# States stored by SP, the sample tile's rows loaded by ScalarE, a product step and a set of masks moved, in a two-layer decoder step

## The reference

```python
for l in range(2):
    h = rmsnorm(x, norm_mix[l]); u, q, k, v, g = split(h @ w_in[l])         # w_in: 1024 x 2560
    pool_out = pool_mix(u, ...)
    s_new = s * gamma**8 + (k * k_decay).T @ v      # per head (4) and sample sequence (8): 128 x 128
    x = x + concat(pool_out, silu(g) * groupnorm(o)) @ w_out[l]
    hf = rmsnorm(x, norm_ffn[l])
    gates = top1_group_then_top2_experts(hf @ w_rg + b, hf @ w_re + b)      # 16 experts
    x = x + sum(gates[:, e] * (silu(hf @ w_gate[e]) * (hf @ w_up[e])) @ w_down[e] for e in range(16))
y = rmsnorm(x, norm_final)
# outputs: y_prompt, y_sample, the pooling buffers, and the retention states of prompt and sample
```

## Time and profile before

| | |
|---|---|
| time, median of 3 runs | 867.52 us (865.8 to 870.74) |
| the profiled execution's own time | 869.52 us |
| its span | 867.7 us |
| mean granted TensorE clock | 0.992 |
| TensorE busy | 843.0 us, 97% of the span |
| VectorE, ScalarE, GpSimd busy | 603.6, 479.4, 316.3 us |
| moved by DMA | 186.29 MB, mean 215 GB/s |

### The profile page before, as it was taken

How to read it: one execution, slowest core, us unless ns; L and a number is a source line. 1 busy time by engine, 2 the same in 40 slices (tenths; PEclk the granted TensorE clock), 3 DMA queues, 4 the chain that set the end, 5 groups by cost and what they waited for, 6 DMA issues and landing times.

```text
span 867.7 us, 12277 instructions
## 1 busy us (share of the span) xinstructions
PE 843.0 (97%) x4254; PEld 671.3 (77%) x4254; DVE 603.6 (70%) x953; ACT 479.4 (55%) x817; POOL 316.3 (36%) x203
## 2 busy tenths in 40 slices
PE   8999999999998999999899999999999999999994
PEld 5787888888866888888478888888877678888851
DVE  3435546555677999998664455655647799999956
ACT  3633442612456888887544333352335498888853
POOL 0014993301021477521100199702101237776110
PEclk9999999999989999999999999999999999999998
DMA  8622222324938999995764222321387698999838
GB/s 292 167 74 81 75 71 85 99 62 145 415 112 307 362 327 388 385 379 207 276 170 157 71 82 62 97 63 61 97 328 285 214 411 307 368 387 382 309 141 285
DMA packets 69439, 186.29 MB, mean 215 GB/s; under 512 B 15724, under 2 KB 26476, under 8 KB 61050
## 3 DMA queue, kind: packets, MB, share of 16 engines
q1 hardware_dynamic: 54714, 151.16, 49.7%
q0 software_dynamic: 10944, 25.19, 8.3%
q10 hardware_dynamic: 3728, 9.26, 2.8%
HBM read 170.56 MB, written 29.91 MB: 231 GB/s over the span
## 4 chain that ended last, share of the span: by engine, by line
PE 86%; DVE 6%; DMA 3%; ACT 2%; issue 1%; SPq 0%; ACTq 0%; POOLq 0%; DVEq 0%
PE ps L420 15%; PE ps L424 11%; PE ps L423 11%; PE ps L1254 9%; PE ps L1256 9%; PE ps L1255 9%; PE ps L422 3%; PE ps L1261 3%; PE ps L1232 2%; PE ps L1456 2%; DMA back<-y_d 1%; PE ps L1396 1%; DMA hg<-xn_d,rowidx 1%; PE ps L1421 1%; PE ps L1267 1%
## 5 line engine op out<-in xcount | busy, mean ns | idle before, releaser
L420 PE MATMUL ps<-wh,hT 128*128 128x512 f32 x480 | 194.0, 404 | 3.3 <-DVE lT L1784 2.6
L758 POOL DMA_INDIRECT y_d<-y,rowidx x32 | 118.5, 3702 | 118.1 <-DVE y L1870 118.1
L1850 DVE TENSOR_TENSOR gul<-wgu,eh 128x1024 fp32r<-128x1024 f32 x128 | 150.3, 1215 | 5.1 <-ACT eh L968 5.0
L424 PE MATMUL ps<-wh,lT 128*128 128x512 f32 x384 | 150.1, 391 | 0.0
L423 PE MATMUL ps<-wl,hT 128*128 128x512 f32 x384 | 150.0, 391 | 0.0
L1841 DVE SCALAR_TENSOR_TENSOR wl<-raw,gcol,wh 128x512 fp32r<-128x512 f32 x80 | 76.8, 964 | 81.4 <-ACT wh L941 81.2
L968 ACT ACTIVATE eh<-wgu 128x1024 fp32r<-128x1024 f32 x128 | 129.0, 1057 | 8.0 <-PE ps L1317 4.5
L420 PEld LDWEIGHTS ps<-wh,hT 128*128 128x128 f32 x480 | 90.3, 188 | 25.2 <-DVE lT L1784 5.2
L1254 PE MATMUL ps<-eh,hgTh 128*128 128x512 f32 x240 | 96.2, 401 | 0.4 <-issue 0.4
L941 ACT ACTIVATE wh<-raw,gcol 128x512 fp32r<-128x512 f32 x80 | 57.4, 721 | 67.9 <-PE ps L422 49.5
L1256 PE MATMUL ps<-eh,hgTl 128*128 128x512 f32 x240 | 93.7, 391 | 0.0
(11 more groups left out here) (231 smaller groups left out, 1577.2 us busy)
## 6 DMA issues: line engine op xcount, KB each, us to landing
wgu<-in_gate_up SPq DMA_DIRECT2D x64, 1024.0 KB, 8.5
wdn<-in_w_down SPq DMA_DIRECT2D x64, 512.0 KB, 12.1
raw<-in_w_in SPq DMA_DIRECT2D x80, 256.0 KB, 2.8
raw<-in_w_out SPq DMA_DIRECT2D x32, 256.0 KB, 3.0
back<-y_d SPq DMA_DIRECT2D x14, 512.0 KB, 7.5
xn_d<-xf ACTq DMA_DIRECT2D x10, 512.0 KB, 4.9
s<-in_state_ret POOLq DMA_DIRECT2D x8, 512.0 KB, 4.8
x<-in_x_prompt SPq DMA_DIRECT2D x4, 512.0 KB, 6.0
```

The costliest lines, as they stand in the source:

```text
L420: pe.matmul(out, both, w_h, start=first, stop=False)
L424: return pe.matmul(out, l[:, t * P:(t + 1) * P], w_h, start=False, stop=final)
L758: pool.indirect_dma_start(out=y_d, out_offset=bass.IndirectOffsetOnAxis(ap=rowidx[:, 1, e:e + 1], axis=0), in_=y[s][:, :], in_offset=None, ...
L1850: ve.tensor_tensor(gu_pair(gul, gul3, e, s, p), gu_pair(wgu, wgu3, e, s, p), eh[p][:, :].bitcast(F32), ALU.subtract).then_inc(glo, 1)
```

## The change

Four moves, no arithmetic added or removed.

- Late steps: their order becomes (2,0), (3,0), (3,1), (2,1). The step (2,1), which stood ahead of the wait for `taken`, comes behind the tables and behind (3,1), on TensorE and on ScalarE. The idle turns become 4 (from 5) ahead of `taken`, and 10 (from 18) behind the last step. SP stores head 3 first, then head 2.
- ScalarE: in the first layer `end_mask(L, 1)` comes behind the rounding of the next layer's blocks 0 to 2 (`w_hi`). VectorE makes the remainders of these blocks ahead of both `sample_state`, which stood around them.
- Last layer: the two row loads of tile 4 are issued by ScalarE behind `back[1]`, and no longer by SP ahead of those of tile 2.
- States of heads 0 and 1: stored by SP behind its row loads, in both layers (behind them in SP's program come, in the first layer, the next layer's blocks 4 and on). GpSimd no longer stores them and no longer waits for tile 2's rows.

```diff
--- before.py
+++ after.py
@@ -492,6 +492,7 @@
         B_Q, B_K, B_SC, B_O, B_KV = 6, 7, 6, 1, 7
         B_OT, B_ON = 0, (4, 5)
         B_END = ((3, 4), (1, 2))
+        LATE_STEPS = ((2, 0), (3, 0), (3, 1), (2, 1))
         B_LATE = ((4, 5), (6, 7))
         B_W = (2, 3, 2, 3, 2, 6, 7, 3, 2, 1, 0, 7, 3, 1, 2)
 
@@ -638,8 +639,8 @@
                     load_gain(NL)
                 sp.wait_ge(xn_st, 16 * NT * (L + 1))
                 sp.wait_ge(lg_mm, 2 * (L + 1))
-                for j in range(2):
-                    sp.wait_ge(s_late, 3 * L + (1, 3)[j])
+                for j in (1, 0):
+                    sp.wait_ge(s_late, 4 * L + (4, 3)[j])
                     sp.dma_start(o["new_ret_sample"][L, :, LATE + j].rearrange("b d e -> d b e"), s_out[j][:, :, :]).then_inc(late_st, 16)
                 for s in range(3):
                     sp.wait_ge(gat[s], 16 * used(L, s, 0))
@@ -681,8 +682,12 @@
                     if L + 1 == NL:
                         t = FINAL[t]
                     i = 2 * t + k
-                    n = tokens(t)
-                    sp.dma_start(back[i][0:n, :], y_d[k * TOK + t * P:k * TOK + t * P + n, :]).then_inc(third_ld if i == 2 else row_ld[t], 16)
+                    if t < LAST or L + 1 < NL:
+                        n = tokens(t)
+                        sp.dma_start(back[i][0:n, :], y_d[k * TOK + t * P:k * TOK + t * P + n, :]).then_inc(third_ld if i == 2 else row_ld[t], 16)
+                for h in range(LATE):
+                    sp.wait_ge(s_new, LATE * L + h + 1)
+                    sp.dma_start(o["new_ret_sample"][L, :, h].rearrange("b d e -> d b e"), s0_end[h][:, :, :]).then_inc(s0_st, 16)
             sp.wait_ge(out_st, 16 * NL)
             sp.wait_ge(upool_st, 32 * NL)
             sp.wait_ge(st_st, 16 * NL)
@@ -834,10 +839,6 @@
                 with pool.Else():
                     pool.wait_ge(t_mm, 2 * NE * (L + 1))
                 pool.wait_ge(t_mm, 2 * NE * (L + 1))
-                pool.wait_ge(row_ld[2], 16 + 32 * (L + 1))
-                for h in range(LATE):
-                    pool.wait_ge(s_new, LATE * L + h + 1)
-                    pool.dma_start(o["new_ret_sample"][L, :, h].rearrange("b d e -> d b e"), s0_end[h][:, :, :]).then_inc(s0_st, 16)
 
         def o_hi(eng, L, t):
 
@@ -901,11 +902,9 @@
 
             def late_state(L, h, n):
 
-                sc.wait_ge(skv_mm, 5 * L + (1 if h == 2 else 2 + n))
-                last = sc.activation(s_out[h - LATE][:, 4 * n:4 * n + 4, :], ps[B_LATE[h - LATE][n]][:, :].rearrange("p (b e) -> p b e", b=4),
-                                     ACT.Copy, scale=float(chunk_decay[1][h]))
-                if h == 3 or n:
-                    last.then_inc(s_late, 1)
+                sc.wait_ge(skv_mm, 6 * L + LATE_STEPS.index((h, n)) + 1)
+                sc.activation(s_out[h - LATE][:, 4 * n:4 * n + 4, :], ps[B_LATE[h - LATE][n]][:, :].rearrange("p (b e) -> p b e", b=4),
+                              ACT.Copy, scale=float(chunk_decay[1][h])).then_inc(s_late, 1)
 
             def gate_diagonals():
 
@@ -1146,7 +1145,6 @@
                 xn_out(L, LAST)
                 gu_hi(L, 0, 0, 0)
                 late_state(L, 2, 0)
-                late_state(L, 2, 1)
                 late_state(L, 3, 0)
                 sc.wait_ge(exp_in, L + 1)
                 sc.activation(gex[:, :, :], gds[:, :, :], ACT.Exp).then_inc(exp_out, 1)
@@ -1154,6 +1152,7 @@
 
                 table(ACT.Silu)
                 late_state(L, 3, 1)
+                late_state(L, 2, 1)
                 sc.wait_ge(xn_st, 16 * NT * (L + 1))
                 rows_hi(L, 0)
                 experts(sc, lambda e, s, n: expert(L, e, s, n))
@@ -1177,16 +1176,19 @@
                 with sc.Else():
                     sc.wait_ge(dpe, 2 * NE * (L + 1))
                 sc.wait_ge(dpe, 2 * NE * (L + 1))
-                end_mask(L, 1)
                 if L + 1 < NL:
                     for s in range(RAW):
                         w_hi(L + 1, s)
-                else:
+                end_mask(L, 1)
+                if L + 1 == NL:
                     table(ACT.Sqrt)
                     gate_diagonals()
                 for s in range(3):
                     sc.wait_ge(y_sc[s], 16 * EUSES[s] * (L + 1))
                 sc.dma_start(back[1][:, :], y_d[TOK:TOK + P, :]).then_inc(second_ld, 16)
+                if L + 1 == NL:
+                    for k in range(2):
+                        sc.dma_start(term(LAST, k)[0:NSAMP, :], y_d[k * TOK + LAST * P:k * TOK + LAST * P + NSAMP, :]).then_inc(row_ld[LAST], 16)
             last_root(0)
             for i, t in enumerate(FINAL):
                 if i + 1 < NT:
@@ -1463,9 +1465,7 @@
                 out, blocks = ps[B_LATE[h - LATE][n]][:, :], slice(4 * n, 4 * n + 4)
                 pe.matmul(out, ident, s0[h][:, blocks, :], start=True, stop=False)
                 pe.wait_ge(vb_done, NH * L + h - LATE + 1)
-                last = pe.matmul(out, kd_late[:, h - LATE, :], vb[h][:, blocks, :], start=False, stop=True)
-                if h == 3 or n:
-                    last.then_inc(skv_mm, 1)
+                pe.matmul(out, kd_late[:, h - LATE, :], vb[h][:, blocks, :], start=False, stop=True).then_inc(skv_mm, 1)
 
             def end_state(L, h):
 
@@ -1567,8 +1567,7 @@
                 logits(L, LAST)
 
                 late_state(L, 2, 0)
-                late_state(L, 2, 1)
-                idle_turns(3, 5)
+                idle_turns(3, 4)
                 pe.wait_ge(taken_done, L + 1)
                 for t in range(NT):
                     for u in range(t + 1):
@@ -1588,7 +1587,8 @@
                     last = pe.matmul(ps[2][:, 0:2 * NE], atslot[:, i, :], name_b[:, i, :, :], start=False, stop=(i == 2 * NT - 1))
                 last.then_inc(tab_mm, 1)
                 late_state(L, 3, 1)
-                idle_turns(3, 18)
+                late_state(L, 2, 1)
+                idle_turns(3, 10)
 
                 pe.wait_ge(gat[0], 16 * used(L, 0, 0))
                 rows_t(0, t_mm)
@@ -2019,7 +2019,7 @@
 
             def sample_state(L, h):
 
-                ve.wait_ge(skv_mm, 5 * L + 3 + h + 1)
+                ve.wait_ge(skv_mm, 6 * L + 4 + h + 1)
                 for n in range(2):
                     v = s0_end[h][:, 4 * n:4 * n + 4, :]
                     last = ve.scalar_tensor_tensor(out=v, in0=v, scalar=float(chunk_decay[1][h]),
@@ -2029,10 +2029,10 @@
             ve.wait_ge(ready0, 4)
             for L in range(NL):
                 if L:
-                    sample_state(L - 1, 0)
                     for s in range(RAW):
                         w_lo(L, s)
-                    sample_state(L - 1, 1)
+                    for h in range(LATE):
+                        sample_state(L - 1, h)
                     for s in range(RAW, EARLY[L]):
                         w_lo(L, s)
                     combine(L - 1, 0, 0)
```

## The result

The changed kernel takes 870.22 us (median of 17 runs, 868.04 to 873.18), the kernel before 867.52 (17 runs, 865.8 to 870.74): ratio 1.0034 [1.0023 to 1.0046], some 2.9 us slower. That is inside the 0.5% and inside the forecast's 863 to 871.5, but 3.1 us above its 867.1 and of the other sign: slower by 2.9, where the forecast had 0.4 faster. The profiled execution took 870.22 us with a span of 868.4; before, 869.52 and 867.7.

A forecast was written before the change was run, and what follows sets the result against it. TensorE was taken to bound the kernel, with 86% of the last-ending chain. End +0.6 (2.5 - 1.9), boundary 0, routing -2.0 or nothing gave 868.1 or 866.1 from the 867.52 median; the middle was 867.1 us, range 863 to 871.5.

The forecast's parts named there:

- Part 1, routing: Late step and turn leave the queue ahead of `taken`: 2.0 us gained in layer 0 at low clock, nothing in layer 1.
- The 1.0 that the number took from it: Routing's mean gain in us, between executions with the low-clock stretch (2.0 gained) and those without it (nothing).
- Part 2, boundary: Between layers, masks behind roundings: rows could come earlier, but idle turns hide the gain; 0, bounds -0.3 and +0.3 us.
- Part 3, the last store: At the end, states stored by SP let the last store land in 3.4 us, not 5.3: -1.9, bounds 0 and -2.6.
- The bounds of the sum for the end: Range given for the end's total, 2.5 - 1.9 = +0.6 us: from -1.3 to +2.5.
- Part 4, tile 4's rows: At the end, tile 4's rows on ScalarE's queue delay tile 3's products by 2.5 us; bounds 0 and 2.7.
- The rival of the low clock: Clock falls in new holes, costing 3.4 us at the end, 2.7 in layer 1's routing; 873.2 for both; chance 0.18.
- if the clock falls in a hole: Stated sign, without a size, that the forecast is wrong: TensorE's clock falling in one of its holes.
- It decides from about there: Low-clock rival's threshold: the clock was down after a 3.3 us hole at the end; the expected hole there was 3.2.
- The other two rivals: At the end: tile 3 not held up, 864.6 us, chance 0.17; last stores not relieved, 869.0 us, chance 0.15.

The follow-up runs named there:

- e2: Changed kernel with 30 idle turns instead of 16 ahead of tile 3's products; 869.26 us, ratio 1.0012 to the kernel before.
- e8: Kernel before with only the late-step reorder and the states stored by SP; 864.47 us, ratio 0.9957 to the kernel before.
- e1: Changed kernel with tile 4's row loads put back on SP's queue, ahead of tile 2's; 865.91 us, ratio 0.9979 to the kernel before.
- e15: Changed kernel itself, measured again in a later group of runs; 870.32 us, ratio 1.0034 to the kernel before.
- e12: Changed kernel with tile 4's rows back on SP and 9 of 25 boundary idle turns moved ahead of head 1's end products; 863.83 us, ratio 0.9956.
- e5: Kernel before with only the states of heads 0 and 1 stored by SP; 868.78 us, ratio 0.9988.
- e6: Kernel before with only tile 4's row loads moved to ScalarE's queue; 871.87 us, ratio 1.0026.
- e13: Kernel before with late-step reorder and SP-stored states, plus SP loading tile 4's rows ahead of tile 3's in the last layer; 868.88 us, ratio 1.0008.
- e3: Kernel before with only late step (2,1) moved behind the tables, with 4 and 10 idle turns; 868.29 us, ratio 0.999.
- e14: Kernel before with late-step reorder and SP-stored states, plus 13 idle turns instead of 4 ahead of positions; 866.42 us, ratio 0.9981.
- e9: Kernel before with only head 1's masks behind three roundings and remainders ahead of both sample states; 869.78 us, ratio 1.0012.

## Why the prediction was wrong in its sign

What failed is the pricing of TensorE's work behind two holes that the change opens. The sum took tile 3's products at the upper clock behind the rows' delay, and between the layers products and turns at 2.0 + 5.6, term 0. Measured, the fallen clock added 1.7 us at the end (`e2`) and some 1.4 at the boundary (`e8` against `e1`, `e15`). Together that is about the 3.1 us between forecast and result. The other differences are smaller and about cancel: the rows 0.8 later than taken, the last landing 0.6 earlier.

**Part 1, routing.** The step was right as drawn: positions came 0.05 behind `taken` (0.1 forecast), the gather 2.4 earlier (2.0), and where the clock was up TensorE had its hole (2.20 against 2.25 forecast). The 1.0 that the number took from it was not refuted: alone the part gave 0.1%, 0.9 us, with zero inside its interval. But it was right, if so, partly by luck. It was the middle between an execution that gains 2.0 and one that gains nothing. In the profiles a routing with the clock up mostly loses 0.8 to 1.5 behind the hole, which was left to a rival, and one with the clock low gains.

**Part 2, boundary.** This step failed. I wrote that masks end at 420.6 and that products and turns follow in 2.0 + 5.6, "Sum 0; bounds -0.3 and +0.3". The place and the order were right (the end products start 8.7 behind the last expert's last products, 8.8 forecast, and the turns took the chain from the rows), but the durations were those of the upper clock. I looked at two holes, and not at the one that this move opens between the 3 turns and the end products, 1.94. Behind it the pair took 9.1 instead of 7.5 in the changed kernel's profile and 10.8 in `e1`'s. `e8` against `e1` puts it at 1.4 us. `e12` shows that it goes when the hole is filled and turns are taken from behind; `e15`'s profile, where the clock stayed up after the same 1.94 and nothing was lost, shows that it is the clock. It fell in four of the five profiles that have this hole, and cost nothing in the fifth.

**Part 3, the last store.** Right in mechanism and nearly in size: 1.9 forecast, 2.3 alone, 2.5 in the changed kernel. Its landing was 2.8, under my 3.4. The medians of `e5` alone don't resolve it. Parts 1 and 3 together gave 0.43% where alone they gave 0.12% and 0.10%; the intervals allow both, so how the gain splits between them stays open. (The bounds of the sum for the end, -1.3 and +2.5, don't follow from those of its terms, which give -2.6 and +2.7; the measured +2.4 is inside both.)

**Part 4, tile 4's rows.** The mechanism was right, the size at the low end: tile 3's products came 3.3 later in the changed kernel's first profile, 2.6 in `e15`'s and 2.5 in `e6`, against the 2.5 taken (2.7 at most). `e13` confirms what the bound was built on, bytes at a low rate ahead of the tile that is wanted. The Trainium skill's rule ("DMA: Bandwidth & Descriptors", Rules for kernel authors) that more issuing engines bring no bandwidth agrees with the runs: 10.3 us with one queue (`e13`), 10.1 with two (`e6`). But the rows' lateness was not the whole price. The forecast moved tile 3's products later and left them at 3.67; they took 5.37, and the last store was issued 4.9 later, not 2.5.

**The rival of the low clock.** It had 0.18 and came true, in both places and in a third, and with it the sign "if the clock falls in a hole". "It decides from about there", 3.3 us, was wrong: holes of 1.9 and 2.2 preceded falls between the layers and in the routing. At the end the hole was 3.3 to 4.0, and the clock fell in each of the five profiles that have it. Its price was too high: 5.37 - 3.67 = 1.7 and not 3.4, because the clock was back after 3.4 us and not 6.7, and in the routing 0.8 to 1.5 and not 2.7. The other two rivals fell: tile 3 was held up, and the last store was relieved.

**The sum.** Forecast: 2.5 - 1.9 + 0 - 1.0 = -0.4. Measured in the places: the end +4.9 - 2.5, the boundary +1.4, the routing about -0.9 (`e3`, 0.1%): +2.9, as the medians have it. The end's terms are from profiles and the others from medians whose intervals are 1 to 2 us either way, so that the exact fit is chance.

## What to carry to other kernels

A move that lets an engine wait opens a hole on TensorE, and what follows must be priced at the lower clock, not only at the durations of the profile before; list every new hole, those between the move and its cover too. Idle turns can cover a late input from ahead of it, in the hole, better than from behind the work that it releases: with nine of 25 moved, part 2's loss of some 1.4 us was gone. That holds where the wait is sure: in the routing, where TensorE is sometimes late itself, nine turns in the hole made the kernel about 2 us slower (`e14`). Before rows go to a second queue, ask which tile is wanted first: here the rows issued beside it delayed it from either queue.

## What the runs showed of the hardware

- Of 14 waits of 1.94 to 2.21 us that the change opens on TensorE (nine ahead of the positions, five ahead of the end products), 12 were followed by a fall to the lower clock; `e15` has 2.20 in both routings with a fall and 1.94 between the layers without one. Behind the older waits of 1.9 to 2.1 us ahead of the transposes, in six profiles without part 2, the clock fell in two (`e13`, `e14`). What tells them apart no run shows.
- A fall that came behind one of these 14 waits, or of the five of 3.3 to 4.0 us at the end, lasted 3.4 us (849.3 to 852.8, 672.1 to 675.6) in 12 cases and 6.8 us in five (`e1` and `e2` between the layers and in layer 1, `e9` between the layers). The shorter ones cost 0.8 to 1.7 us on the chain, the longer ones 1.5 in the routing and some 3 between the layers (21.0 to 21.3 against the 18.0 of `e15`). Of the kernel before, executions apart by 0.005 in mean granted clock were 4.2 us apart.
- A 0.5 MB pair of 64-row loads, issued beside or ahead of full tiles, delayed the tile behind it by 2.5 to 3.3 us, where 0.52 MB at the 403 GB/s of the earlier trace rows is 1.3.
- Taking two state stores from beside the last output stores shortened the last landing from 5.3 to 2.8 us (2.9 in `e5` and `e8`).
